# Filler products in TensorE's waits, and three quarters of one expert weight group loaded early in layer 1

## The reference

```python
for i in range(DEPTH):
    h  = modulate(rmsnorm(x,  norm1_g[i]), sh1,  sc1)     # shift and scale from silu(c) @ mod_w[i] + mod_b[i]
    hc = modulate(rmsnorm(xc, norm1_g[i]), sh1c, sc1c)
    m, mc = mixer_ab(...) if i % 2 == 0 else mixer_cd(...)
    x = x + g1 * m
    h = modulate(rmsnorm(x, norm2_g[i]), sh2, sc2)
    x = x + g2 * expert_choice_ffn(h, moe_router[i], moe_w1[i], moe_w3[i], moe_w2[i])
    if not last:                                          # the context stream is dropped in the last layer
        xc = xc + g1c * mc
        ...
def expert_choice_ffn(h, router_w, w1, w3, w2):
    aff = softmax(h @ router_w)
    gates, idx = top_k(swapaxes(aff, 1, 2), cap)          # cap = 32 tokens for each of 16 experts
    xe = take(h, idx)
    hid = silu(xe @ w1) * (xe @ w3)
    ye = (hid @ w2) * gates                               # added back at idx
```

## Time and profile before

| | |
|---|---|
| Median of 3 runs | 2329.61 us (2329.37 to 2329.66) |
| The profiled execution's own time | 2330.99 us |
| Its span, first to last instruction | 2329.3 us |
| Mean granted TensorE clock | 0.932 of full speed |
| Busy: PE, DVE, ACT, POOL | 1957.6, 721.7, 504.4, 165.1 us |
| Moved by DMA | 527.21 MB, mean 226 GB/s |

### The profile page before, as it was taken

How to read it: one execution, slowest core, us unless ns; L and a number is a source line. 1 busy time by engine, 2 the same in 40 slices (tenths; PEclk the granted TensorE clock), 3 DMA queues, 4 the chain that set the end, 5 groups by cost and what they waited for, 6 DMA issues and landing times.

```text
span 2329.3 us, 29832 instructions
## 1 busy us (share of the span) xinstructions
PE 1957.6 (84%) x12790; PEld 1011.5 (43%) x12790; DVE 721.7 (31%) x1306; ACT 504.4 (22%) x1072; POOL 165.1 (7%) x208
## 2 busy tenths in 40 slices
PE   6999789999997988888888899989998776666655
PEld 2444544445443333333335565567887521212112
DVE  2221543345214001010116775656774300000001
ACT  2442212234102100000013233354442100000001
POOL 0000000020000000000004000044440000000000
PEclk9999889999998999999999999999998877878788
DMA  9012021150115999999992423300002499999996
GB/s 385 36 72 107 38 110 73 72 217 1 37 72 253 413 430 431 431 430 430 430 417 89 171 119 153 128 20 2 2 2 81 172 384 430 429 432 432 430 432 259
DMA packets 34211, 527.21 MB, mean 226 GB/s; under 512 B 2336, under 2 KB 3616, under 8 KB 17952
## 3 DMA queue, kind: packets, MB, share of 16 engines
q1 hardware_dynamic: 32464, 522.55, 53.3%
q10 hardware_dynamic: 1616, 2.76, 0.3%
HBM read 524.26 MB, written 1.05 MB: 226 GB/s over the span
## 4 chain that ended last, share of the span: by engine, by line
PE 46%; DMA 31%; DVE 8%; issue 6%; PEld 5%; ACT 3%; DVEq 1%; PEldq 1%; ACTq 0%; SPq 0%; POOL 0%
DMA ring<-in_moe_w 28%; PE bank L523 13%; PE bank L1073 10%; PE bank L983 5%; PEld bank L523 4%; PE bank L944 2%; DVE ring L1911 2%; PE bank L748 1%; PE bank L725 1%; DMA ring<-in_mod_w 1%; DMA ring<-in_cd_w 1%; DVE x L2320 1%; PE bank L575 1%; DVE x L1749 1%; PE bank L673 1%
## 5 line engine op out<-in xcount | busy, mean ns | idle before, releaser
L523 PE MATMUL bank<-hT,ring 128*128 128x512 f32 (+1 forms) x1504 | 554.1, 527 | 21.2 <-DMA ring<-in_cd_w 10.5
L1073 PE MATMUL bank<-ring,xgs 128*32 128x512 f32 x3072 | 395.0, 669 | 140.3 <-DMA ring<-in_moe_w 138.8
L523 PEld LDWEIGHTS bank<-hT,ring 128*128 128x128 f32 x1504 | 286.5, 193 | 269.1 <-issue 235.7
L1073 PEld LDWEIGHTS bank<-ring,xgs 128*32 128x32 f32 x3072 | 110.7, 121 | 398.6 <-issue 298.4
L1073 PE MATMUL bank<-ring,hT 128*32 128x512 f32 x1488 | 199.1, 691 | 76.9 <-DMA ring<-in_moe_w 76.9
L2161 DVE SCALAR_TENSOR_TENSOR x<-bank,modT,x 128x256 f32<-128x256 f32 x96 | 42.4, 481 | 468.6 <-PE bank L1099 468.6
L1073 PEld LDWEIGHTS bank<-ring,hT 128*32 128x32 f32 x1488 | 56.1, 124 | 206.7 <-issue 165.1
L1749 DVE SCALAR_TENSOR_TENSOR x<-gluR,cols,x 128x256 f32<-128x256 f32 x240 | 116.0, 483 | 16.2 <-issue 0.4
L2150 DVE TENSOR_TENSOR hT<-mrow,bank 128x512 f32<-128x512 f32 x16 | 10.9, 684 | 191.2 <-PE bank L1073 191.2
L2150 DVE TENSOR_TENSOR hT<-small,bank 128x512 f32<-128x512 f32 x8 | 5.5, 688 | 178.7 <-PE bank L1073 178.7
L1494 ACT ACTIVATE xgs<-bank 128x512 f32<-128x512 f32 x24 | 14.3, 597 | 209.7 <-PE bank L1056 209.7
(11 more groups left out here) (476 smaller groups left out, 2296.0 us busy)
## 6 DMA issues: line engine op xcount, KB each, us to landing
ring<-in_moe_w SPq DMA_DIRECT2D x94, 4096.0 KB, 22.5
ring<-in_mod_w SPq DMA_DIRECT2D x12, 4096.0 KB, 13.5
ring<-in_cd_w SPq DMA_DIRECT2D x6, 4096.0 KB, 18.3
ring<-in_ab_w SPq DMA_DIRECT2D x4, 4096.0 KB, 21.1
ring<-in_ab_wo SPq DMA_DIRECT2D x2, 4096.0 KB, 14.9
ring<-in_cd_wo SPq DMA_DIRECT2D x2, 4096.0 KB, 13.4
early<-in_moe_w SPq DMA_DIRECT2D x2, 2048.0 KB, 21.8
ring<-in_moe_w SPq DMA_DIRECT2D x2, 2048.0 KB, 17.8
```

The lines of the kernel that those rows point to most:

```text
L523: last = mm(ps[p["no"] % 4][:, p["c0"]:T], w[:, k, :], hT[:, k, p["c0"]:T], start=(k == 0), stop=(k == KD - 1))
L1073: last = mm(ps[banks + s][32 * j:32 * j + 32, :], lhs[s][:, 4 * kh + k, 32 * j:32 * j + 32], w[:, 4 * k + j, :], start=(kh == 0 and k == 0 ...
```

## The change

A helper `keep_warm(n, bank)` issues n products of the identity with itself, 128x128x128, into a bank whose contents nobody needs then. Calls of it are put ahead of waits on TensorE: 14 between the halves of the first modulation, 3 and 6 around its turn, 10 or 4 ahead of each turn in GLA except the first, 13 and 5 in GDN's first iterations, up to 4 at each hand-off of its last, 2 + 26 + 10 in the route of layer 0 and 16 + 6 + 26 + 6 in that of layer 1. In GLA six more products, of zeros with the identity and added to the open output bank, stand ahead of the wait for the states. In layer 1 three quarters of group 3 (3 MB) go into the stream-0 halves of the four expert buffers, issued with `early`; after product 0 only its last quarter is loaded into the ring, and group 3's product takes each piece from where it lies.

```diff
@@ -292,9 +294,16 @@
                 n = first + gi
                 if gi == RING:
                     sp.wait_ge(sg("x_ready"), 2 * layer + 1)
+                    if layer:
+                        for b in range(2):
+                            sp.dma_start(xgs[:, b, 0, :, :].rearrange("p k c -> p (k c)"),
+                                         A["moe_w"][layer, gi, :, 1024 * b:1024 * b + 1024]).then_inc(spare_in, 16)
+                        sp.dma_start(htok[:, 0:2, :].rearrange("p t n -> p (t n)"), A["moe_w"][layer, gi, :, 2048:4096]).then_inc(spare_in, 16)
+                        sp.dma_start(pick[:, 0, :, :].rearrange("p a c -> p (a c)"), A["moe_w"][layer, gi, :, 4096:5120]).then_inc(spare_in, 16)
+                        sp.dma_start(gateT[:, 0, :, :].rearrange("p q c -> p (q c)"), A["moe_w"][layer, gi, :, 5120:6144]).then_inc(spare_in, 16)
                     sp.dma_start(early[:, :], A["moe_w"][layer, last, :, 0:4096]).then_inc(early_in, 16)
                 sp.wait_ge(w_used, n - RING + 1)
-                k0 = 4096 if gi == last else 0
+                k0 = 4096 if gi == last else 6144 if layer and gi == RING else 0
                 sp.dma_start(ring[:, n % RING, :, :].rearrange("p j n -> p (j n)")[:, k0:8192],
                              A["moe_w"][layer, gi, :, k0:8192]).then_inc(landed[n % RING], 16)
 
...
@@ -429,6 +438,11 @@
             def group_in(n):
                 pe.wait_ge(landed[n % RING], rg.landed[n])
 
+            def keep_warm(n, bank):
+
+                for _ in range(n):
+                    mm(ps[bank][:, 0:P], ident[:, :], ident[:, :], start=True, stop=True, skip_group_check=True)
+
...
@@ -437,6 +451,8 @@
                 else:
                     pe.wait_ge(sg("mod_row_copied"), 3 * layer + r)
                 for kh in range(2):
+                    if layer == 0 and r == 0 and kh == 1:
+                        keep_warm(14, 0)
                     group_in(first + kh)
                     w = slot(first + kh).rearrange("p g (k n) -> p g k n", k=4)
                     for k in range(4):
...
@@ -541,6 +557,8 @@
             def gla():
                 def turn_and_match(n, d):
 
+                    if n:
+                        keep_warm(4 if d else 10, 0)
                     pe.wait_ge(sg("gla_gated"), n + 1)
                     for t in range(NT):
...
@@ -567,6 +585,8 @@
                            g_v[:, bass.ds(2 * h, 2), t, :], start=(d == 0 and t % 2 == 0), stop=False, skip_group_check=True)
                     if more:
                         turn_and_match(n + 1, 1 - d)
+                    for _ in range(6):
+                        mm(ps[6][:, 0:P], zero[:, :], ident[:, :], start=False, stop=False, skip_group_check=True)
                     pe.wait_ge(sg("gla_S"), n + 1)
                     for c in range(NC):
                         if c == (0 if d == 0 else 3):
...
@@ -769,6 +789,8 @@
 
                     if n >= KD:
                         return
+                    if n == 0:
+                        keep_warm((10, 3)[d], 0)
                     pe.wait_ge(sg("gdn_Kt"), 2 * n + 1)
                     pe.wait_ge(sg("gdn_E"), 2 * n + d + 1)
                     for t in range(NT):
...
+                def fill(it, n):
+
+                    if it == KD:
+                        keep_warm(n, 0)
+
                 for it in range(-1, KD + 1):
                     p, s, n = it, it - 1, it + 1
+                    if it == 0:
+                        keep_warm(5, 0)
                     level_r(p, 1)
                     new_values(s, 0)
+                    fill(it, 4)
                     spread(n, 0)
                     conformer_sum(it, range(2))
                     level_p(p, 1)
                     state_step(s, 0)
+                    fill(it, 2)
                     spread(n, 1)
                     conformer_sum(it, range(2, 4))
                     level_r(p, 2)
                     state_out(s, 1)
+                    fill(it, 2)
...
@@ -1013,6 +1051,8 @@
                                                        hT[:, 4 * half + k, t * P:(t + 1) * P], ident[:, :])
                         last.then_inc(sg("htok_turned"), 1)
 
+                if layer:
+                    keep_warm(16, 5)
                 pe.wait_ge(sg("router_in"), 16 * (layer + 1))
                 for k in range(KD):
                     pe.wait_ge(sg("h_ready"), 8 * (2 * layer + 1) + k + 1)
...
                         turn_tokens(i, t)
+                keep_warm(6 if layer else 2, 5)
                 pe.wait_ge(sg("affinities"), 2 * layer + 1)
                 for tt in range(2):
                     last = nc.tensor.transpose(ps[3][0:48, tt * P:(tt + 1) * P], affc[:, tt, :], ident[:, :])
                 last.then_inc(sg("aff_turned"), 1)
+                keep_warm(26, 5)
                 pe.wait_ge(sg("affinities"), 2 * layer + 2)
                 for tt in range(2):
                     last = nc.tensor.transpose(ps[4][:, 48 * tt:48 * tt + 48], pickw[:, 1, tt * P:(tt + 1) * P], ident[0:48, 0:48])
...
 
+                def piece(g, n, i):
+
+                    if g == 12 * Q - 1 and i < 8:
+                        return early[:, 512 * i:512 * i + 512]
+                    if layer and g == RING and i < 4:
+                        return xgs[:, i // 2, 0, 4 * (i % 2):4 * (i % 2) + 4, :].rearrange("p k c -> p (k c)")
+                    if layer and g == RING and i < 8:
+                        return htok[:, (i - 4) // 2, 512 * (i % 2):512 * (i % 2) + 512]
+                    if layer and g == RING and i < 12:
+                        return pick[:, 0, i - 8, :] if i < 10 else gateT[:, 0, 2 * (i - 10):2 * (i - 10) + 2, :].rearrange("p q c -> p (q c)")
+                    return ring[:, n % RING, :, :].rearrange("p a (b n) -> p (a b) n", b=4)[:, i, :]
+
                 def product(q, gi, kh, lhs, banks):
-                    n = first + 12 * q + gi
-                    w = ring[:, n % RING, :, :].rearrange("p a (b n) -> p (a b) n", b=4)
-                    split = 12 * q + gi == 12 * Q - 1
+                    g = 12 * q + gi
+                    n = first + g
+                    if g == 12 * Q - 1:
+                        pe.wait_ge(early_in, 16 * (layer + 1))
+                    if layer and g == RING:
+                        pe.wait_ge(spare_in, 80)
                     for k in range(4):
-                        if split and k == 0:
-                            pe.wait_ge(early_in, 16 * (layer + 1))
-                            w = early[:, :].rearrange("p (a n) -> p a n", n=512)
-                        if k == (2 if split else 0):
+                        if k == (2 if g == 12 * Q - 1 else 3 if layer and g == RING else 0):
                             pe.wait_ge(landed[n % RING], rg.landed[n])
-                            w = ring[:, n % RING, :, :].rearrange("p a (b n) -> p (a b) n", b=4)
                         for s in streams:
                             for j in range(4):
                                 last = mm(ps[banks + s][32 * j:32 * j + 32, :], lhs[s][:, 4 * kh + k, 32 * j:32 * j + 32],
-                                          w[:, 4 * k + j, :], start=(kh == 0 and k == 0), stop=(kh == 1 and k == 3),
...
@@ -1115,6 +1168,7 @@
                     last.then_inc(sg("gates_turned"), 1)
 
                 ns = len(streams)
+                keep_warm(6 if layer else 10, 5)
                 pe.wait_ge(sg("picks"), 2 * layer + 1)
                 pe.wait_ge(sg("htok_copied"), 8 * layer + 4 * ns)
                 for b in range(ns):
...
@@ -1170,7 +1224,10 @@
 
             pe.wait_ge(consts_made, 1)
             norm(T)
-            modulation(0, 0)
+            modulation_rows(0, 0)
+            keep_warm(3, 0)
+            modulation_turn(0, 0)
+            keep_warm(6, 0)
             project(PLAN["gla"], gates=gla_gate, ready=0)
             pe.wait_ge(sg("gla_zeroed"), 1)
             pe.wait_ge(sg("proj_evacuated"), len(PLAN["gla"]))
```

More of the change, by code:

```diff
@@ L912, in gdn @@
                     state_out(s, 2)
+                    fill(it, 1)
                     turn_queries(n)
```

8 lines of the change are left out of this document (added).

## The result

The changed kernel takes 2312.39 us in the median of 4 runs (2311.43 to 2313.9), the kernel before 2329.64 us beside it (2329.37 to 2330.97): a ratio of 0.9921, 95% interval 0.9909 to 0.9933, so 0.8% faster; the medians lie 17.2 us apart. The forecast was 2308.5 us with a range of 2300 to 2318. Of the runs further down, two executions of e1 ran at 2670 and 2673 us with a granted clock of 0.74 and 0.73, and are left out of its ratio.

A forecast was written before the change was run, and what follows sets the result against it. The prediction took the DMA queue to bound the expert stages, and a chain through TensorE, partly at its lower clock, to set their start. Terms summing to -21.1 from the median of 2329.61 gave 2308.5 us, range 2300 to 2318.

The forecast's parts named there:

- Start: First modulation: 14 fillers fit in the wait for weights and the second half falls to 3.64 us: -1.6 us.
- GLA with its modulation rows: Gated linear attention: faster last products and modulation rows, less a loss of 4.2 in odd directions: -4.7 us in all.
- rival A: The clock still falls in GLA, losing 8.9 us of gain while the loss of 4.2 stays: 2317.4 us, chance 0.20.
- Route of layer 0: Layer 0's routing: gather at 3.84 instead of 6.59 us, two fillers costing +0.5: -2.3 us in all.
- GDN's first iteration: Gated DeltaNet, first iteration: fillers hidden behind ScalarE, L776 and L796 at the upper clock level: -1.8 us.
- Last iteration: Gated DeltaNet, last iteration: five quartets of L837 on the state's chain save 0.5 us each: -2.6 us.
- Output projection's start: After GDN: a gain of 0 to 1.6 us if the clock stays up there, left out of the sum.
- Route of layer 1: Layer 1's routing: logits -1.0, gather -1.7, product 0 -2.0: -4.7 us in all.
- Spare 3 MB: Layer 1's experts: early loading gains 3.4 us; about 4 of the 7.3 become a queue pause.
- B: Fillers run at the lower clock level, 0.47 us each, and outlast their waits: 2367 us, chance 0.03.
- C: Fillers cost 0.15 us or less, so GLA's odd directions lose nothing: 2304.3 us, chance 0.17.
- D: The spare pieces bring nothing because product 3 or another group is then waited for: 2311.9 us, chance 0.05.

The follow-up runs named there:

- e1: The changed kernel with every filler count at 0 and the spare 3 MB kept: 2327.63 us, ratio 0.9988 to the kernel before.
- e11: The kernel before, unchanged, traced a second time: 2336.82 us in one run.
- e6: The kernel before with 27 fillers added in layer 0's experts and nowhere else: 2332.3 us, ratio 1.0004 to the kernel before.
- e4: The changed kernel with the spare 3 MB taken as one quarter of group 3 and two of group 4: 2308.08 us, ratio 0.9909.
- e7: The kernel of e4 with 24 fillers added in layer 0's experts: 2307.73 us, ratio 0.9896 to the kernel before.
- e10: The kernel of e4 with 36 fillers added in layer 0's experts: 2306.56 us, ratio 0.9891 to the kernel before.
- e5: The changed kernel with 24 fillers added in layer 0's experts: 2310.03 us, ratio 0.9912 to the kernel before.
- e2: The changed kernel with its fillers kept and no spare pieces loaded: 2316.54 us, ratio 0.995 to the kernel before.
- e3: The changed kernel without the fillers of GLA's odd directions that have a successor: 2312.19 us, ratio 0.9923 to the kernel before.
- e8: The changed kernel with each filler product made one transpose, the zero fillers staying products: 2316.33 us, ratio 0.9935 to the kernel before.

## Why the prediction was right, point by point

- **Start:** -1.6 forecast, -1.40 measured; against e11 it would be -5.0, against e6, with the code of before there, -0.1.
- **GLA with its modulation rows:** -4.7 forecast, -5.84 measured (-4.16 and -1.68). All eight L595 are at 1.94, so rival A's price didn't come. Its reason did in part: 2.0 to 2.1 us stay idle before L564 in even directions, and the clock fell behind that in one of them, for 0.6 us; in e4, e7 and e10 it fell in three, and the stage is 1.4 us longer. The term that was mis-sized is the loss in odd directions: +0.84 each instead of +1.4. The ten fillers there took 2.23 us and the six 1.43 (3.66 instead of 3.84), L564 and L567 1.33 instead of 1.55; that is 0.4 of the 0.56 missing.
- **Route of layer 0:** -2.3 forecast, -2.34 measured. **GDN's first iteration:** -1.8 forecast, -1.63 measured; in e5 and e7 1.4 us of it are lost again, where L768 in the second iteration takes 1.97 us and 1.15 in the changed kernel. **Last iteration:** -2.6 forecast, -2.56 measured.
- **Output projection's start:** 0 to -1.6 was left out; it came, -1.29 (L982 10.96 us instead of 12.24).
- **Route of layer 1:** -4.7 forecast, -5.11 measured: logits -1.33 (5.27 to 3.95), gather -1.74, product 0 -1.93.
- **Spare 3 MB:** -3.4 forecast; -4.38 in the changed kernel's trace, -3.3 in e1, and -3.45 as the difference to e2 (441.99). So the term itself held. The rest is the last product of the kernel, 8.68 us instead of 9.90; e3 and e8, with fillers too, have 9.95 and 10.01 there, so that is again where the clock falls, and no term of the sum. At the upper level the product would take 7.07.
- **Unforeseen, +5.0:** "the experts of layer 0 keep their length and move with it" failed, by +2.19, and the projection of layer 1, which the sum didn't name, by +2.80. The two late loads are 1.12 + 1.27 = 2.4 of the latter, through instruction fetches that the fillers shifted. Of the former 1.56 is a product at the lower clock: "TensorE's clock is worth nothing inside them" fails for the last products of an expert stage, behind which no load is waited for. Against e11 the two stages are only 0.85 and 0.97 us longer. Rows of before would have allowed the question: its queue of fetches is on the page, and the time of each in the trace.

The gains were 3.5 us larger than forecast and 5 were given back, so that the sum missed the trace by only 1.6 (-19.56 for -21.1) and the median by 3.9 us (2312.39 for 2308.5). A part of the agreement is luck: errors of both signs met, and with e11 as the trace of before the difference would have been 25.4 instead of 19.6. Rivals B and C fell with the filler's 0.22 to 0.24 us, D with e1.

## What to carry to other kernels

Filling TensorE's waits pays where its next instruction is on the path, and nowhere else. In a stage bound by the queue the last product is such a place: an estimated 1.6 us were left at each of the two here (15.5 against 13.94, 8.68 against 7.07), and no run filled the wait ahead of them. Where fillers also delay the product behind them, these runs don't tell whether they pay. A change that adds instructions moves the instruction fetches of everything behind it: after such a change compare the issue-to-landing time of each load that the path waits for, and look for a fetch inside it; here 24 more fillers in covered waits (96 instructions) moved one fetch out, and 36 both. Take a second trace of the kernel before, and only then put a stage's difference down to the change. When a prefetch ends before its ring slot comes free, spread it over the next two transfers rather than take more of one.

## What the hardware showed that I had not expected

- A 16 KB instruction fetch inside a 4 MB load on the path: landing 13.95 to 14.45 us after the issue, against 12.70 to 12.97, in 28 of 28 loads, and only one of a load's 16 parts is late.
- The granted clock falls at places that differ from execution to execution of the same program (second modulation half 5.23 or 6.25 us, and 3.64 in e6 at identical code there); with fillers it still fell in GLA, behind 2.0 to 2.1 us of idle time, in one to three of four even directions (GLA 92.1 to 93.6 us).
- Transposes hold the granted clock at 1.00 as products do, if they fill the same time; one took 0.125 us against 0.24 for a float32 product of 128 columns.
